# Expert weights in three buffers instead of two, the first 16 passes written out, first requests moved

## The reference, cut to what matters

```
probs = softmax(x @ router_w)
group  = argmax over 4 groups of (sum of the 2 best of probs + bias)
expert = the 2 best experts in the group;  w = their probs, normed to sum 1
hid = silu(x @ w_gate[e]) * (x @ w_up[e])          # 1024 -> 512, per chosen expert
y   = sum over the 2 experts of w * (hid @ w_down[e])   # 512 -> 1024
```

## Time and profile before

| | us |
|---|---|
| median of 3 runs | 1583.6 (1581.77 to 1587.2) |
| the profiled execution, its own time | 1588.11 |
| its span | 1586.3 |
| PE busy | 1295.7 (82%) |
| DVE, ACT, POOL busy | 450.5, 381.3, 183.6 |
| granted TensorE clock, mean | 0.917 |

### The profile page before, as it was taken

The page is one execution under the profiler, slowest core; times in us unless marked ns, Lnnn a source line. Parts: engine busy times, 40 slices in busy tenths (PEclk is TensorE's granted clock), DMA queues, the critical chain, the costliest instruction groups (busy, mean ns, idle before and its releaser), DMA issues. The chain is left out here.

```text
span 1586.3 us, 18584 instructions
## 1 busy us (share of the span) xinstructions
PE 1295.7 (82%) x6770; PEld 753.6 (48%) x6770; DVE 450.5 (28%) x1204; ACT 381.3 (24%) x990; POOL 183.6 (12%) x226
## 2 busy tenths in 40 slices
PE   3798998998996964986888868999999298787883
PEld 1376767776775532332222335687774133232232
DVE  0544345444433151110011134323322411101014
ACT  1234434443441120110011113222223111111011
POOL 0021101110110003111111000111100211111100
PEclk8999999999998986998899979999999599999896
DMA  9554223421322074999999962533302689999983
GB/s 387 221 219 176 110 92 151 176 110 68 123 110 105 5 292 158 396 405 398 415 406 396 420 261 122 170 102 128 96 7 120 246 312 399 406 410 406 403 344 129
DMA packets 50226, 372.90 MB, mean 235 GB/s; under 512 B 8460, under 2 KB 24180, under 8 KB 29940
## 3 DMA queue, kind: packets, MB, share of 16 engines
q1 hardware_dynamic: 43700, 359.47, 57.1%
q0 software_dynamic: 6464, 12.61, 2.4%
HBM read 362.49 MB, written 16.90 MB: 239 GB/s over the span
## 5 line engine op out<-in xcount | busy, mean ns | idle before, releaser
L1943 PE MATMUL bank<-slot,scr 128*64 128x512 f32 x608 | 306.7, 663 | 92.4 <-DMA slot<-in_w_u 90.5
L1945 PE MATMUL bank<-slot,scr 128*64 128x512 f32 x608 | 306.6, 663 | 0.0
L1943 PEld LDWEIGHTS bank<-slot,scr 128*64 128x64 f32 x608 | 88.7, 152 | 282.3 <-issue 182.9
L2045 DVE TENSOR_TENSOR scr<-scr,bank 64x512 f32<-64x512 f32 x38 | 26.2, 690 | 417.6 <-ACT scr L2010 417.6
L662 PE MATMUL bank<-hnP,slot 128*128 128x387 f32 x384 | 138.8, 510 | 1.3 <-issue 1.3
L1962 PE MATMUL bank<-slot,scr 128*64 128x512 f32 x304 | 138.4, 598 | 1.0 <-DVE scr L2050 1.0
L1964 PE MATMUL bank<-slot,scr 128*64 128x512 f32 x304 | 138.5, 598 | 0.0
L2010 ACT ACTIVATE scr<-bank 64x512 f32<-64x512 f32 x38 | 22.4, 591 | 381.6 <-PE bank L1945 381.6
L662 PEld LDWEIGHTS bank<-hnP,slot 128*128 128x128 f32 x384 | 73.7, 200 | 48.0 <-issue 9.2
L1336 PE MATMUL bank<-yT,slot 128*128 128x384 f32 x256 | 86.3, 498 | 6.1 <-DMA slot<-in_w_out 4.7
L1945 PEld LDWEIGHTS bank<-slot,scr 128*64 128x64 f32 x608 | 88.7, 152 | 0.0
(11 more groups left out here) (309 smaller groups left out, 1842.2 us busy)
## 6 DMA issues: line engine op xcount, KB each, us to landing
slot<-in_w_g SPq DMA_DIRECT2D x38, 2048.0 KB, 17.9
slot<-in_w_u SPq DMA_DIRECT2D x38, 2048.0 KB, 23.6
slot<-in_w_d SPq DMA_DIRECT2D x38, 2048.0 KB, 24.5
slot<-in_ada_w SPq DMA_DIRECT2D x24, 2048.0 KB, 12.9
slot<-in_gdn_w SPq DMA_DIRECT2D x8, 2048.0 KB, 9.2
slot<-in_mlstm_w SPq DMA_DIRECT2D x8, 2048.0 KB, 8.1
slot<-in_w_out SPq DMA_DIRECT2D x2, 4096.0 KB, 15.2
slot<-out_d SPq DMA_DIRECT2D x6, 1024.0 KB, 7.0
```

The lines of the kernel that those rows point to most:

```text
L1943: gate = nc.tensor.matmul(bank[0:CAP, 0, :], x, w_gate[par][:, k, :], start=(k == 0), stop=(k == KD - 1))
L1945: up = nc.tensor.matmul(bank[CAP:2 * CAP, 1, :], x, w_up[par][:, k, :], start=(k == 0), stop=(k == KD - 1))
```

## The change

- `slot`, hnP, yT, hnT and scr become parts of one tensor `big`, in this order. `w_exp` looks at its first nine pieces of 2 MB as three buffers of gate, up, down. Buffers 0 and 1 are the old six pieces; buffer 2 lies over hnP, yT, hnT and the start of scr (htok).
- Pass p < 16 uses buffer p mod 3. These 16 passes are written out on all engines with constant waits. Passes 16 and on run in a `Fori`, two per turn, in the buffers 1 and 0 alternately. There is always at least one pass of more than 16 (made even to two).
- SP requests gate and up of pass p (3 to 15) when gate_up(p-3) is done, then w_down of pass p when down(p-3) is done, in this order for each p. In the loop: gate and up of pass q when gate_up(q-2) is done, then w_down of pass q when down(q-2) is done.
- First requests. Layer 0: gate and up of expert 0 right behind `w_out` in head 7; at `delta_mm` w_down 0, the three pieces of expert 1, gate 2; then the writes of `hn_d`; then up 2 (needs the last transposes) and, when the writes have landed, w_down 2. Layer 1: `w_out` goes to pieces 3 and 4 and is requested behind the rows of heads 0 and 1, and gate and up of expert 16 (expert 0 of this layer) right behind it; its w_down when head 6 has used its weights; the rest as in layer 0.
- PE waits for the outputs of pass p-2 ahead of down(p-1), no longer at the end of a turn. One more gather pair, one more turn_tokens and its copies run at the end (of a list with no tokens). POOL waits for the last gathers.
- Two semaphores of the mLSTM are replaced by others; `pass_f` loses its first 16 columns; one small copy is added to fill the empty lists.

The core of the diff:

```
-        slot = sb("slot", [P, 6, SLOT])
+        big = sb("big", [P, 6 * SLOT + KD * (PAD + 2 * T) + SCR])
+        slot = big[:, 0:6 * SLOT].rearrange("p (s n) -> p s n", s=6)
+        w_exp = big[:, 0:BUFS * 3 * SLOT].rearrange("p (b w n) -> p b w n", b=BUFS, w=3)
...
                     wout_sync(sp, 0)
+                    gate_up_in(sp, 0, 0, 0)
...
-        WOUT_AT = (2, 0)
+        WOUT_AT = (2, 3)
...
-            sp.wait_ge(delta_mm, 2 * KD)
-            wout_sync(sp, 1)
             sp.wait_ge(gate_dve, G0 + 2)
...
             rows_and_states(0)
             rows_and_states(1)
+            sp.wait_ge(cols_mm, 2)
+            wout_sync(sp, 1)
+            sp.wait_ge(delta_mm, 2 * KD)
+            gate_up_in(sp, 1, E, 0)
             for h in range(H):
                 if h + 2 < H:
                     sp.wait_ge(m_vz_ps, NT * (h + 1))
                     mlstm_weights_sync(sp, h + 2)
+                elif h + 1 < H:
+                    sp.wait_ge(m_vz_ps, NT * (h + 1))
+                    down_in(sp, 1, E, 0)
...
+            for p in range(E):
+                gate_up(p, p % BUFS, loaded(layer, p))
+                turn_tokens(p + 1, (p + 1) % 2)
+                if p > 1:
+                    outputs_taken(p - 2)
+                if p > 0:
+                    down(p - 1, (p - 1) % BUFS, loaded(layer, p - 1))
+                turn_hidden(p, p == 0)
+
+            with pe.Fori(0, more, 2) as i:
+                gate_up(i + E, EVEN, i // 2 + 6)
+                turn_tokens(i + (E + 1), 1)
+                outputs_taken(i + (E - 2))
+                down(i + (E - 1), ODD, i // 2 + 6)
+                turn_hidden(i + E)
+                gate_up(i + (E + 1), ODD, i // 2 + 7)
+                turn_tokens(i + (E + 2), 0)
+                outputs_taken(i + (E - 1))
+                down(i + E, EVEN, i // 2 + 6)
+                turn_hidden(i + (E + 1))
+            outputs_taken(more + (E - 2))
+            down(more + (E - 1), ODD, more // 2 + 6)
...
+        def moe_first_sync(sp, layer):
+
+            x = layer * E
+            sp.wait_ge(delta_mm, KD * (2 * layer + 1))
+            if layer == 0:
+                down_in(sp, layer, x, 0)
+            gate_up_in(sp, layer, x + 1, 1)
+            down_in(sp, layer, x + 1, 1)
+            gate_up_in(sp, layer, x + 2, 2, ("w_g",))
+            route_sync(sp, layer)
+            sp.wait_ge(e_tr, 3 * layer + 3)
+            gate_up_in(sp, layer, x + 2, 2, ("w_u",))
+            sp.wait_ge(e_hn_out, 16 * NT * (layer + 1))
+            down_in(sp, layer, x + 2, 2)
+
+        def moe_sync(sp, layer, more):
+            e = moe[layer]
+            for p in range(BUFS, E):
+                sp.wait_ge(e["up"], 2 * (p - 2))
+                gate_up_in(sp, layer, layer * E + p, p % BUFS)
+                sp.wait_ge(e["y_ps"], 2 * (p - 2))
+                down_in(sp, layer, layer * E + p, p % BUFS)
+
+            with sp.Fori(0, more, 2) as i:
...
+                for j, buf in enumerate((EVEN, ODD)):
+                    wait_turn(sp, e["up"], i * 2 + (2 * E - 2 + 2 * j), e_place, 3 * layer + 3)
+                    gate_up_in(sp, layer, xs[j], buf)
+                    wait_turn(sp, e["y_ps"], i * 2 + (2 * E - 2 + 2 * j), e_place, 3 * layer + 3)
+                    down_in(sp, layer, xs[j], buf)
```

More of the change, by code:

```diff
@@ L46 @@
 N_PASSES = E + MAX_MORE
+BUFS = 3
 FAR = 1 << 20
@@ L1980, in moe_pe, with moe_act @@
             turn_tokens(0, 0)
[L1981 to L2001, removed]
+            for p in range(E):
[19 more added lines that the diff above has]
+            down(more + (E - 1), ODD, more // 2 + 6)
+        def moe_act(act, layer, more):
             e = moe[layer]
@@ L2021, in moe_act, with moe_dve @@
             tokens(0)
[L2022 to L2025, removed]
+            for p in range(E):
                 gate(p)
                 tokens(p + 1)
-                out(p - 1)
+                if p > 0:
+                    out(p - 1)
                 hidden(p)
-            gate(n - 1)
-            out(n - 2)
-            hidden(n - 1)
-            out(n - 1)
-        def moe_dve(dve, layer, n):
+            with act.Fori(0, more) as i:
+                gate(i + E)
+                tokens(i + (E + 1))
+                out(i + (E - 1))
+                hidden(i + E)
+            out(more + (E - 1))
+        def moe_dve(dve, layer, more):
             e = moe[layer]
@@ L2052, in moe_dve @@
             tokens(0)
-            product(0)
-            tokens(1)
-            with dve.Fori(1, n - 1) as p:
+            for p in range(E):
                 product(p)
                 tokens(p + 1)
-                out(p - 1)
-            product(n - 1)
-            out(n - 2)
-            out(n - 1)
+                if p > 0:
+                    out(p - 1)
+            with dve.Fori(0, more) as i:
+                product(i + E)
+                tokens(i + (E + 1))
+                out(i + (E - 1))
+            out(more + (E - 1))
         def moe_start_pool(pool, layer):
@@ new lines, in moe_pool @@
+            for p in range(E - 2):
+                pool.wait_ge(e["xp"], p + 3)
+                gather(p + 4, p % 2, 2 * p + 5)
+                scatter(p, 2 * p + 6)
+            with pool.Fori(0, more, 2) as i:
+                for j in range(2):
+                    wait(e["xp"], i + (E + 1 + j))
+                    gather(i + (E + 2 + j), j, i * 2 + (2 * (E - 2) + 2 * j + 5))
+                    scatter(i + (E - 2 + j), i * 2 + (2 * (E - 2) + 2 * j + 6))
+            for j in range(2):
+                scatter(more + (E - 2 + j), more * 2 + (2 * E + 1 + j))
@@ L2216, in _ @@
             gdn_sync(sp)
-            sp.wait_ge(delta_mm, KD)
             moe_first_sync(sp, 0)
@@ L2253, in _ @@
                 route_pe(pe, layer)
-                n = passes(pe, layer)
+                more = passes(pe, layer)
                 pe.wait_ge(e_expl, layer + 1)
-                moe_pe(pe, layer, n)
-                pe.wait_ge(moe[layer]["y_sb"], n * 2)
+                moe_pe(pe, layer, more)
+                pe.wait_ge(moe[layer]["y_sb"], more * 2 + 2 * E)
                 combine_pe(pe, layer)
```

169 lines of the change are left out of this document (76 added, 93 removed).

## The result

The changed kernel took 1594.3 us (median of 11 runs; nine lie from 1588.1 to 1597.4, and the comparison leaves out the other two, which are far above) against 1583.6 for the kernel before in the same session. The ratio of the runs compared is 1.0059 [1.0038, 1.0079], the brackets being the 95% interval: 9.3 us slower. The forecast was 1580, 3.5 us faster, with a range of 1567 to 1592.

A forecast was written before the change was run, and what follows sets the result against it. The prediction took weight transfers landing before the last gate_up, and their queue running dry, to bound the passes. Passes -8.6, mLSTM +5.1 and routing 0 gave -3.5 us on a median of 1583.6: 1580, range 1567 to 1592.

The forecast's parts named there:

- written-out code: Passes written out instead of looped: at most 2 x 0.95 us better per layer by the skill's rule, taken as 0.
- extra turn_tokens: End of each layer, between gate_up and down 18: one more turn_tokens costs +1.0 us per layer.
- the loop's queue: Passes over 16: DMA's queue mostly stays filled; +1 us per layer, between 0 and 3.25 for each late pass.
- margin of 1.2 us: Loop passes: the queue still holds 4.5 us of work when a fresh request needs 3.25, so it doesn't run dry.
- rival C: Loop passes: the queue runs dry in every pass, each losing up to 3.25 us; slower, 1592 us; chance 0.13.
- one of the signs: Passes of the loop: DMA's share falling below 1.0 there would show the prediction wrong.
- The routing: Token lists after `delta_mm`: layer 0 costs 0 to 1.4 us, layer 1 gains 0 to 1.4, together 0.
- The start gap: Start of each layer's passes: w_down 3 waits for down(0) and finds a dry queue, +3.4 us.
- Two pieces fewer, not three: End of each layer: down 18 now precedes up 19, so two pieces of 4.85 us are saved, 9.7 us.
- Rival B: Passes: the whole pass is won, with no gap at the start; 1559.5 us; chance 0.06.
- The mLSTM: Head 2's weights land behind four other pieces: 3.9 us wait plus 1.3 us slower clock, +5.1 us.
- The passes as a whole: Passes of both layers: -4.3 us each from pieces saved, start gap, loop and extra turn_tokens, -8.6 us together.

The follow-up runs named there:

- e7_two: Changed kernel's layout and written-out code, but requests as in the kernel before (two passes ahead; only layer 1's `w_out` later): 1593.3 us, 1.0047 of the kernel before.
- e6_loop: Changed kernel with gate and up of the next pass requested ahead of w_down only for w_down 15 and the loop: 1575.3 us, 0.9942 of the kernel before.
- e4_routing: Changed kernel with pass 2's w_up and w_down requested behind the first turn_tokens in both layers: 1592.9 us, 1.0053 of the kernel before.
- e10_best: Changed kernel: next gate/up ahead of w_down, `w_out` and expert 16's gate/up behind head 2's weights, layer 0's pass 2 up/down after routing: 1564.3 us, 0.9877 of before.
- e11_two_edits: Changed kernel with next gate/up ahead of w_down, and `w_out` and expert 16's gate/up behind head 2's weights: 1566.2 us, 0.9892 of the kernel before.
- e3_order: Changed kernel with gate and up of pass p+1 requested ahead of w_down of pass p in all passes: 1574.5 us, 0.9938 of the kernel before.
- e8_layout: Kernel before with only the changed kernel's memory layout, five tensors in one: 1587.7 us, 1.0023 of the kernel before.

## Why the prediction was wrong

The sum was -3.5 us, the measurement +9.3. The difference is 12.8, and `e7_two` splits it. Layout, written-out code and extra turn_tokens without the new requests are +7.4 us [4.6, 10.3], where the prediction had 2.0 (the turn_tokens alone): 5.4 too little. The rest of the change, the third buffer with its requests, is 1.0059 - 1.0047, +1.9 us, where the prediction had -5.5: 7.4 too little. The first half is known to within 3 us, the second to within 4. Two steps failed most: the written-out code taken as 0 with the layout not priced, and the loop's queue taken as 1 us a layer. Step by step:

1. **Written-out code, 0; the memory layout, not priced at all.** Wrong: +8.6 us for both [1.0054], in the kernel before without turn_tokens or new requests. The argument, that the row with 0.95 us ended by DVE leaves no room, bounds only what written-out code can give, not what it can cost. The Trainium skill's rule in "Runtime: NRT & Kernel Launch", section "Instruction fetch mechanics", that unrolling spares a taken branch's stall, pointed the other way; here writing out 15 passes cost 0.30% and 0.46%. Why is open, for both parts.
2. **The loop's queue, +1.0 a layer.** Too small: by DMA's share 7.8 us for both layers in the profile against 2.0, six passes with 1.3 us each. The margin of 1.2 us was worked out with a down that ends 12 us after its gate_up begins, and with a fallen clock as the exception. Measured in layer 0 it is 14.2 and 14.4 us in every second pass, since PE came back from the idles of 5.29 and 5.13 us with the lower clock; the prediction's own limit was 13.25. It also supposed that two passes stay queued until pass 15. At the turn from three buffers to two this fails: gate and up 16 must wait for gate_up(14), and the third buffer's lead is given back there (836.5 to 860.5 without a request). This is rival C's mechanism, and DMA's share below 1.0 in the loop is one of the signs that the prediction named as proving it wrong. C's evidence against itself, "nearly the same distance in the old loop", was misread: the old loop had gate and up ahead of w_down, so a late w_down held nothing up. `e6_loop`, which reorders the late requests alone, wins 1.2%.
3. **The routing, 0 with bounds of 1.4.** Wrong in layer 0: the lists come 3.4 us later. The bound was made from when the pieces end, 603 before and 604.7 after; it left out that the small scatters are served beside 2 MB pieces requested as late as 596.2. In `e4_routing`, without two of these pieces, the lists take 24.5 us and not 29.4. The expected -1.4 of layer 1 didn't come either (24.5 and 23.9 us). How much of the 3.4 us reaches the end isn't shown: `e10_best` against `e11_two_edits` returns 1.9 at the median and 0.5 in the stages of layer 0.
4. **The start gap, +3.4 a layer.** Too large: it was priced against a queue that never rests, but the kernel before has shares of 0.94 and 1.01 where the changed one has 0.87 and 0.97. The difference is 1.05 + 0.6 = 1.65 us in layer 0, and 0.75 + 1.05 = 1.8 in layer 1 (0.95 and 1.01 against 0.90 and 0.99, over 15 and 51.5 us). `e3_order` against `e6_loop` returns 0.6 us for both layers. Steps 2 and 4 together are 7.8 + 3.4 = 11.2 us against their 8.8.
5. **Two pieces fewer, not three: -9.7.** The price of a piece holds. With gate and up p+1 ahead of w_down p the third piece is won too, and the nearest pair with the same code and layout, `e7_two` (two passes ahead) and `e11_two_edits`, has passes of 590.3 and 562.2 us: 28.1 us, and six pieces at 4.85 are 29.1. At the medians it is 1.0047 - 0.9892 = 1.55%, 24.5 us, the early requests included. Rival B's price was right, for an order that the change didn't have. That the changed kernel's own order wins just two is not measured by itself.
6. **The mLSTM, +5.1.** Right in mechanism and place (L1418 in the new numbering), 3.98 us of wait against 3.9 and 1.8 of clock against 1.3. At the median it is more: 1.0062 - 0.9993 is 0.7%, 11 us with an interval of about 4, and 0.9938 - 0.9892 is 7 us in the other pair. In the stages it is 6.1 and 6.2 us.
7. **The passes as a whole, -8.6.** They came out at -7.6 in the profile, partly by luck. With what was measured for its terms it is -19.4 for four pieces, +7.8 and +3.4 for the dry queue, and +2.5 for code, layout and turn_tokens (590.3 in `e7_two` against 587.8): -5.7, within 2 us of it. A right total is no proof of its terms.

What the profiles can't show is that two executions of equal time, 1588.1 us, have medians 10.7 us apart: one lies 4.5 us above its median, the other 6.2 below. Within most of the kernels the longer executions show the lower granted clock. The changed kernel's profiled one has 0.921, the highest of its nine; its three longest (1596.2 to 1597.4) have 0.909 to 0.913. The spread is no matter of the dry queue: the layout alone, with no dry queue, ranges over 14 us (1579.8 to 1593.9). Which of clock and time moves the other is not shown.

Open: why the layout costs 0.23 to 0.37%, where it does, by what the written-out passes lose 4 us while their DMA share stays at 1.01, and what part the lower clock has in both.

## What to carry to other kernels

In a queue that is served in order, write for each request the moment its own condition is met beside the moment it is issued; the request whose condition comes last goes last. A further buffer is worth the pieces that leave the critical stretch (here 4.85 us each) only if the order behind it doesn't hand them back, most of all where the kernel returns to fewer buffers. Work out a margin at the engine's slower clock too, where it comes behind a wait. Price as well the code and layout that a change needs: written-out loops and a moved layout cost as much here as a stall, and they can be run alone in the old kernel before the rest is built.

## What the runs showed of the hardware that was not expected

- Small indirect scatters beside 2 MB pieces requested up to 596.2 were done 3.4 us later than beside pieces requested up to 584.9 (7.9 against 4.5 us from the last scatter to the read that waits for them).
- In the late passes of layer 0 the matmuls after an idle of 5.29 and 5.13 us ran at the lower clock (1.06 instead of 0.59 us), those after 1.64 and 0.98 us did not. So a wait of PE in one pass delayed the request that followed, by 2.3 to 2.5 us.
- Placing five tensors in one allocation, with no instruction changed otherwise, cost 0.23% and 0.37% on two chips.
- Writing out 15 of the passes raised the instruction queue from 0.64 to 0.87 MB and the time by 0.30% and 0.46%.
- The kernel before, against itself, read 0.9990 [0.9976, 1.0005], while its single executions range over 0.6% (1578.2 to 1587.9). In its 18 runs beside `e8_layout` the shortest (1580.1 us) had a granted clock of 0.924, the longest (1589.0) 0.916.
